# Feed-forward activations on other engines: square on ScalarE, low half on GpSimd, weight subtraction in four pieces

## The reference

```python
def post_norm_block(h, mix, ln1_g, ln1_b, w_ff_up, w_ff_down, ln2_g, ln2_b):
    h = layer_norm(DEEPNORM_ALPHA * h + mix, ln1_g, ln1_b)
    ff = jnp.square(jax.nn.relu(h @ w_ff_up)) @ w_ff_down
    return layer_norm(DEEPNORM_ALPHA * h + ff, ln2_g, ln2_b)
```

## Time and profile before

| | |
|---|---|
| median of three runs | 3179.45 us (3174.3 to 3191.85) |
| profiled execution | 3178.85 us |
| its span in the trace | 3176.9 us, 42244 instructions |
| mean granted TensorE clock | 0.924 |
| busy: PE, PEld, DVE, ACT, POOL | 2779.1, 2407.3, 1488.3, 654.4, 569.1 us |

### The profile page before, as it was taken

The page is one execution under the profiler, slowest core; times in us unless marked ns, Lnnn a source line. Parts: engine busy times, 40 slices in busy tenths (PEclk is TensorE's granted clock), DMA queues, the critical chain, the costliest instruction groups (busy, mean ns, idle before and its releaser), DMA issues.

```text
span 3176.9 us, 42244 instructions
## 1 busy us (share of the span) xinstructions
PE 2779.1 (87%) x15803; PEld 2407.3 (76%) x15803; DVE 1488.3 (47%) x2861; ACT 654.4 (21%) x1156; POOL 569.1 (18%) x264
## 2 busy tenths in 40 slices
PE   3968999948999999958889996879899999999996
PEld 3968889948888899845556654769887878788884
DVE  5057999982455545123333425421634343434336
ACT  2033211102233344111223323210310000001011
POOL 4201122210100000100000000122421222222223
PEclk9979999979999999978889968889899999999998
DMA  4142322213211111155434334241111111111001
GB/s 180 56 103 55 105 93 86 85 44 90 76 56 53 31 45 40 55 147 152 143 106 141 113 111 146 99 160 36 39 40 40 40 40 40 40 40 40 26 26 56
DMA packets 173658, 244.03 MB, mean 77 GB/s; under 512 B 49889, under 2 KB 147330, under 8 KB 164146
## 3 DMA queue, kind: packets, MB, share of 16 engines
q1 hardware_dynamic: 139890, 204.03, 20.0%
q10 hardware_dynamic: 33600, 37.80, 3.5%
HBM read 180.00 MB, written 59.08 MB: 75 GB/s over the span
## 4 chain that ended last, share of the span: by engine, by line
PE 65%; DVE 20%; issue 6%; ACT 3%; DMA 2%; SPq 2%; DVEq 2%; POOL 1%; ACTq 0%; POOLq 0%; PEldq 0%
PE ps L955 6%; DVE masks L1694 6%; PE ps L1218 4%; PE ps L1219 4%; PE ps L1220 4%; PE ps L1238 4%; PE ps L1240 3%; PE ps L1239 3%; PE ps L835 2%; DVE maskS L1694 2%; PE ps L836 2%; PE ps L837 2%; PE ps L1059 2%; PE ps L943 2%; PE ps L757 2%
## 5 line engine op out<-in xcount | busy, mean ns | idle before, releaser
L411 POOL TENSOR_TENSOR pool_go<-pool_go 128x1 f32<-128x1 f32 x73 | 15.1, 207 | 2498.0 <-PE ps L837 780.3
L414 POOL TENSOR_TENSOR w_lo<-raw,w_hi 128x2048 fp32r<-128x2048 f32 x73 | 352.8, 4833 | 10.9 <-issue 0.5
L1238 PE MATMUL ps<-w_hi,a_hi 128*128 128x512 f32 (+1 forms) x576 | 241.6, 419 | 66.9 <-DVE res L2080 60.2
L835 PE MATMUL ps<-xt_hi,w_hi 128*128 128x368 f32 x768 | 260.9, 340 | 0.7
L2080 DVE TENSOR_TENSOR res<-res,ps 128x512 f32<-128x512 f32 (+1 forms) x270 | 181.7, 683 | 169.3 <-PE ps L1240 169.3
L1218 PE MATMUL ps<-xt_hi,w_hi 128*128 128x368 f32 x768 | 254.3, 331 | 3.4 <-SPq L368 3.4
L836 PE MATMUL ps<-xt_lo,w_hi 128*128 128x368 f32 x768 | 257.3, 335 | 0.0
L837 PE MATMUL ps<-xt_hi,w_lo 128*128 128x368 f32 x768 | 256.4, 334 | 0.0
L1219 PE MATMUL ps<-xt_lo,w_hi 128*128 128x368 f32 x768 | 254.6, 332 | 0.0
L1220 PE MATMUL ps<-xt_hi,w_lo 128*128 128x368 f32 x768 | 254.1, 331 | 0.0
L1240 PE MATMUL ps<-w_lo,a_hi 128*128 128x512 f32 (+1 forms) x576 | 236.5, 411 | 0.0
(11 more groups left out here) (286 smaller groups left out, 6348.4 us busy)
## 6 DMA issues: line engine op xcount, KB each, us to landing
raw<-w_stream SPq DMA_DIRECT2D x73, 1024.0 KB, 5.0
kpg<-cache_k SPq DMA_DIRECT2D x128, 128.0 KB, 2.2
qT_d<-kT ACTq DMA_DIRECT2D x48, 184.0 KB, 1.9
gate_d<-kT ACTq DMA_DIRECT2D x48, 184.0 KB, 1.9
gst<-gate_d SPq DMA_DIRECT2D x16, 552.0 KB, 5.7
gvog_d<-kT ACTq DMA_DIRECT2D x64, 128.0 KB, 1.9
qraw<-qT_d SPq DMA_DIRECT2D x64, 128.0 KB, 3.1
vpg<-cache_v ACTq DMA_DIRECT2D x64, 128.0 KB, 2.5
```

The costliest lines, as they stand in the source:

```text
L414: pool.tensor_tensor(w_lo[:, s, :], raw[:, s, :], w_hi[:, s, :].bitcast(F32), ALU.subtract).then_inc(w_split, 1)
L835: pe.matmul(out, hi, xt_hi[:, k, cols], start=k == 0, stop=False)
L1238: pe.matmul(out, a_hi[:, a, k, cols], w_hi[:, s, w], start=k == 0, stop=False)
```

## The change

Three edits. The square of the Relu block moves from VectorE to ScalarE, between a drain on either side, and the semaphore `f_sq` goes. The low half `a_lo` moves from VectorE to GpSimd, where the loop over weight units is written out so that a low half follows each split. In `split`, which serves all 73 units, the subtraction is issued as four instructions of 512 columns in place of one of 2048; the last one counts `w_split` up. VectorE's feed-forward loop is left with the 18 sums.

```diff
-        f_relu, f_sq, f_hi, f_lo, f_half, f_add = (
-            sem(n) for n in ("f_relu", "f_sq", "f_hi", "f_lo", "f_half", "f_add"))
+        f_relu, f_hi, f_lo, f_half, f_add = (
+            sem(n) for n in ("f_relu", "f_hi", "f_lo", "f_half", "f_add"))
...
                 pool.drain()
-                pool.tensor_tensor(w_lo[:, s, :], raw[:, s, :], w_hi[:, s, :].bitcast(F32),
-                                   ALU.subtract).then_inc(w_split, 1)
+                for c in range(4):
+                    part = slice(512 * c, 512 * c + 512)
+                    last = pool.tensor_tensor(w_lo[:, s, part], raw[:, s, part], w_hi[:, s, part].bitcast(F32),
+                                              ALU.subtract)
+                last.then_inc(w_split, 1)
...
-            for u in (U_FF + 1, U_FF + 2):
-                split(u % 2, 16 * (u // 2) + 16, u - 1)
-            split_units(U_FF + 3, N_UNITS - 1)
-            split(0, 16 * (N_UNITS // 2) + 16, N_UNITS - 2)
+
+            def low(a, c, his):
+                pool.wait_ge(f_hi, his)
+                pool.tensor_tensor(a_lo[:, a, c, :], rl[:, c, :], a_hi[:, a, c, :].bitcast(F32),
+                                   ALU.subtract).then_inc(f_lo, 1)
+
+            split(0, 16 * ((U_FF + 1) // 2) + 16, U_FF)
+            low(0, 0, 1)
+            split(1, 16 * ((U_FF + 2) // 2) + 16, U_FF + 1)
+            low(0, 1, 2)
+            low(1, 0, 3)
+            split(0, 16 * ((U_FF + 3) // 2) + 16, U_FF + 2)
+            low(1, 1, 4)
+            with pool.Fori(0, (FB - 2) // 2) as i:
+                for o in range(2):
+                    u = U_FF + 4 + 2 * o
+                    split(1, 32 * i + (16 * (u // 2) + 16), 4 * i + (u - 1))
+                    low(o, 0, 4 * i + (5 + 2 * o))
+                    split(0, 32 * i + (16 * ((u + 1) // 2) + 16), 4 * i + u)
+                    low(o, 1, 4 * i + (6 + 2 * o))
...
-            def hidden(a, halves, units, lows, squares, used):
+            def hidden(a, halves, units, lows, used):
                 for c in range(2):
                     chunk_ready(c, halves, units)
                     if lows is not None:
                         act.wait_ge(f_lo, lows + c)
                     act.activation(rl[:, c, :].rearrange("p (n m) -> p n m", m=N3), ps[:, 3 * c:3 * c + 3, 0:N3],
                                    ACT.Relu).then_inc(f_relu, 1)
-                    act.wait_ge(f_sq, squares + c)
+                    act.drain()
+                    act.activation(rl[:, c, :], rl[:, c, :], ACT.Square)
+                    act.drain()
                     if used is not None:
                         act.wait_ge(unit_done, used)
                     act.activation(a_hi[:, a, c, :], rl[:, c, :], ACT.Copy).then_inc(f_hi, 1)
...
-            for j in range(2):
-                for c in range(2):
-                    square(c, 2 * j + 1)
-                    low(c, j, 2 * j + 1)
             sums(0, 18, 1, U_FF + 3, True)
             with dve.Fori(0, (FB - 2) // 2) as i:
                 for o in range(2):
-                    n = 4 * i + (5 + 2 * o)
-                    square(0, n)
-                    low(0, o, n)
-                    hv, uv = 34 * i + 17 * (o + 1) + 1, 4 * i + (U_FF + 5 + 2 * o)
-                    square(1, n)
-                    sums(0, 2, hv, uv)
-                    low(1, o, n)
-                    sums(2, 18, hv, uv)
+                    sums(0, 18, 34 * i + 17 * (o + 1) + 1, 4 * i + (U_FF + 5 + 2 * o))
```

More of the change, by code:

```diff
@@ L1565, in _ @@
             hb = halves_before(U_FF)
-            hidden(0, hb + 1, U_FF + 1, None, 1, None)
-            hidden(1, hb + 2, U_FF + 2, 1, 3, None)
+            hidden(0, hb + 1, U_FF + 1, None, None)
+            hidden(1, hb + 2, U_FF + 2, 1, None)
             with act.Fori(0, (FB - 2) // 2) as i:
@@ L1570, in _ @@
                     hidden(o, 2 * i + (hb + 3 + o), 4 * i + (U_FF + 4 + 2 * o), 4 * i + (3 + 2 * o),
-                           4 * i + (5 + 2 * o), 4 * i + (U_FF + 3 + 2 * o))
+                           4 * i + (U_FF + 3 + 2 * o))
             norm(2, res)
@@ L2057, in _ @@
             barrier(dve, 8)
[L2060 to L2066, removed]
             def sums(m0, m1, halves, units, first=False):
```

## The result

The changed kernel took 3078.93 us (median of 4 runs, 3073.72 to 3088.43) beside 3176.88 us for the kernel before: a ratio of 0.9683, with a 95% interval of 0.9648 to 0.9717. It is faster, by 98 us; the forecast was 3070 us in a range of 3052 to 3095. The profiled execution took 3073.72 us (span 3071.8), 105.1 us less than that of the kernel before, of which the working foresaw 109.

What follows compares the result with a forecast made beforehand. TensorE was taken to wait for VectorE's sums, queued behind operations that GpSimd's instructions hold. Gains of 92 + 12 + 5 = 109 us off the profiled 3178.85 gave 3070 us, range 3052 to 3095.

Steps and rivals of the forecast that it cites:

- Term 1: Feed-forward part: with square and low half off VectorE, TensorE no longer pauses and passes fall to 49.16 us; 92 us gained.
- the rival that only the waits would go: Feed-forward part: short pauses and the low clock stay, so only 58.5 us go there; 3118 us in all, chance 0.10.
- The cover: Feed-forward part: ScalarE and GpSimd have room for the moved work, costed at nothing; without it some 3 us a half pass.
- The main rival: Threshold search and early operations: VectorE cannot start between GpSimd's undrained pieces, so nothing is gained there; 3087 us, chance 0.30.
- Term 2: Threshold search: VectorE's held operations start between pieces of `w_lo`; 12 us gained, ends 0 and 25.
- I take half: Threshold search: 18.8 us for six stalls of L1711, halved to 9.4 because shifted passes give most of it back.
- Term 3: Two early operations right before TensorE's start of a stage, L1646 3.2 us sooner and L1631 1.9; together 5 us, ends 0 and 8.
- The slower-by-the-clock rival: Feed-forward loop: 688 us of matmuls without pause get 1.2 GHz for a share; at a quarter 3242 us, chance 0.05.

## Why the prediction was right, and where it was not

**Term 1, 92 us: right, 91.2.** Passes of 49.2 us at a clock of 1.00, as worked out from the undisturbed up unit and the steady down tile; the rival that only the waits would go (58.5 us) falls. The prices held: `a_lo` 2.58 us (2.56 forecast), four pieces 5.03 to 5.07 (5.12), Square 1.13 (1.13). The first down product gained 8.5 us by the ledger (8.4). The cover held too: GpSimd waits for `a_hi` 144.2 us in all, before 16 of its 32 low halves, and for TensorE before its splits, and nothing waits for GpSimd.

The Trainium skill's advice against element-wise work on GpSimd (GPSIMD Engine Reference, § 4.1) describes the price rightly, 2.58 us against 1.31, and not its weight here: the low half alone, moved there, gained 70 us.

**The main rival, that pieces let nothing in: wrong.** The `kiS` operation at 2.04 us, the low half at 2.38 in the kernel with pieces alone, and the barrier waits that fall with the size of the pieces each show VectorE taking its turn between two pieces that nothing separates. The 0.06 us by which GpSimd's instructions overlap in the trace was no evidence of a hold. By this the trace agrees with the Trainium skill, SBUF — State Buffer, § SBUF: two separate sides, that the lock lasts for one instruction; the warning in the Trainium skill's GPSIMD Engine Reference, § 2.1, did not decide.

**Term 2, 12 us: the direction right, the size half of the 23.2 measured.** The failed step is "I take half": it assumed that shifted passes give half of the six long stalls back. They give back a quarter. The six small operations of the 31 passes fell from 72.5 to 56.0 us together: the 128x7 `take` by 18.5, as the working had it before halving, `low_m` by 3.5, while `cut` and the other `take` rose by 5.5 between them. What remains of the 22 us at the barrier, 5.5, came in the steps that build the masks behind each loop, which the term did not count (the first `eqb` 4.82 us before and 0.36 now, a scan 6.30 and 2.99, against some that grew).

**Term 3, 5 us: the size right by luck, the operations wrong.** 5.1 us were gained by the last split of the search, but 3.0 of them at a normalisation product (L1604, 5.41 us beside `w_lo` before, 2.17 now), which the prediction did not name, and 0.6 stood before the first split, where nothing had changed. Both operations that it named became shorter: L1646 by 3.2 us as forecast, L1631 from 3.30 to 0.16 us, more than forecast. But the transfer of `ki_p` took the first gain, and behind the second the barrier waited 2.04 us for SP's queue: the step missed that a DMA, not VectorE, would be last there. The other profiles with four pieces have 6 to 9 us at that split.

**Not in the sum: -17 us of half clock.** The slower-by-the-clock rival looked at the feed-forward loop, where the clock stayed at 1.00. The clock was lost in a stage that the change only shifts in time. Its argument that the low stretches follow a pause does not cover the kernel before itself, which has 51 us at 0.50 from 1833 us on with no wait over 0.3 us in the 13 us ahead of it. So the total of 109 against 105 is partly chance: 11 us too little in the search and 17 too much for a stage taken as unchanged. Which head gets a stretch of the second kind, and why, stays open.

## What to carry to other kernels

Where VectorE's operations on SBUF are late, look at what GpSimd runs just then: cutting its long instructions into pieces gives VectorE an opening at each cut, here at some 0.16 us for each, and moving the held operation off VectorE gives all of it. A gain is only banked when the stages behind it keep their pace: compare the start of one recurring instruction in both traces from stage to stage, and a loss far from the edit shows at once. Keep a bulk load out from between small stores whose buffers are needed again at once; where TensorE does not come to wait for them, as in the kernel before, this gains nothing.

## What the runs showed of the hardware

A pause of 1.83 us was followed by 33 us at 0.50 of the clock, nine times its own length in lost time, and so were four more of 1.28 to 1.48 us in the same stage; yet the 1.14 us pauses in each pass of the feed-forward loop with only the square left on VectorE went with a granted clock of 1.00, a pause of 3.11 us in that loop with only the low half left there (at 2498 us) was followed by only 3 to 4 us at 0.50, and a head ran 51 us at 0.50 behind no wait longer than 0.8 us. So the length of the pause alone does not tell what follows. The hold between VectorE and GpSimd is mutual and begins anew at each instruction: four pieces took 5.03 us alone, 5.93 with one VectorE operation let in and 6.97 beside a square and a low half.
